# Sparse attention's distance biases stored 128 times and loaded row by row, the selection mask added to them on GpSimd

## What is computed

```python
score = jnp.einsum('bqh,bqhs->bqs', wi_b, s_idx)             # which keys are worth a look
score = jnp.where(causal[None], score, -jnp.inf)
_, sel = lax.top_k(score, topk)                              # 64 keys per query
bias = rel_bias[t5_bucket(jnp.maximum(dist, 0))]             # (distance q - k) -> 8 heads
logits = einsum('bqhc,bqkc->bqhk', qa_b, lat_sel) + moveaxis(bias, -1, 2)
p = softmax(where(valid, logits, -inf)); out = einsum('bqhk,bqkc->bqhc', p, lat_sel)
```

## Time and profile before

| | |
|---|---|
| time, three runs | 1334.58, 1338.58, 1341.36 us (median 1338.58) |
| the profiled execution | 1332.08 us, its span 1330.2 us |
| busy over the span | PE 1218.4 us (92%), POOL 895.9 (67%), ACT 587.5 (44%), DVE 464.8 (35%) |
| DMA | 196.60 MB, mean 148 GB/s; HBM written 1.06 MB |
| granted TensorE clock | mean 0.98 |

### The profile page before, as it was taken

The page is one execution under the profiler, slowest core; times in us unless marked ns, Lnnn a source line. Parts: engine busy times, 40 slices in busy tenths (PEclk is TensorE's granted clock), DMA queues, the critical chain, the costliest instruction groups (busy, mean ns, idle before and its releaser), DMA issues.

```text
span 1330.2 us, 19675 instructions
## 1 busy us (share of the span) xinstructions
PE 1218.4 (92%) x7628; PEld 1033.3 (78%) x7628; DVE 464.8 (35%) x834; ACT 587.5 (44%) x859; POOL 895.9 (67%) x913
## 2 busy tenths in 40 slices
PE   2998999999999999998989898898998989999997
PEld 2897987777677888788978886666778977788775
DVE  6476447643343111004265552332234032211101
ACT  2463234135536454445533335535456344644532
POOL 0689245314595888785966665468879966788785
PEclk9999799999999999999999999899999999999999
DMA  8755222323554566564633333235545634555562
GB/s 326 200 164 141 65 69 92 97 80 111 172 164 149 181 189 190 174 188 113 190 111 101 114 119 110 81 127 159 190 147 153 198 119 143 156 181 186 174 189 97
DMA packets 182909, 196.60 MB, mean 148 GB/s; under 512 B 7416, under 2 KB 141856, under 8 KB 182688
## 3 DMA queue, kind: packets, MB, share of 16 engines
q1 hardware_dynamic: 178336, 186.56, 45.5%
q10 hardware_dynamic: 4480, 8.78, 2.1%
HBM read 194.25 MB, written 1.06 MB: 147 GB/s over the span
## 4 chain that ended last, share of the span: by engine, by line
PE 72%; DVE 10%; POOL 6%; ACT 6%; issue 4%; DMA 1%; POOLq 0%; ACTq 0%; DVEq 0%; SPq 0%
PE ps L621 19%; PE ps L623 18%; PE ps L622 18%; PE ps L618 14%; POOL wlo L2421 6%; PE ps L626 3%; DVE hE L1693 3%; DMA raw<-in_ada_w 1%; ACT hE L1183 1%; ACT L1183 1%; ACT whi L1183 1%; DVE gt L1693 1%; DVE x L1701 1%; DVE AD L2254 1%; DVE acc L1701 0%
## 5 line engine op out<-in xcount | busy, mean ns | idle before, releaser
L2421 POOL TENSOR_TENSOR wlo<-raw,whi 128x256 fp32r<-128x256 f32 (+1 forms) x904 | 890.4, 1018 | 419.2 <-ACT whi L1183 415.0
L1183 ACT ACTIVATE whi<-raw 128x1024 fp32r<-128x1024 f32 x325 | 341.5, 1056 | 353.2 <-PE ps L623 330.5
L621 PE MATMUL ps<-whi,hThi 128*128 128x512 f32 (+2 forms) x672 | 270.0, 402 | 9.7 <-POOL wlo L2421 4.3
L623 PE MATMUL ps<-whi,hTlo 128*128 128x512 f32 (+2 forms) x672 | 261.2, 389 | 0.0
L622 PE MATMUL ps<-wlo,hThi 128*128 128x512 f32 (+2 forms) x672 | 260.8, 388 | 0.0
L621 PE MATMUL ps<-hThi,whi 128*128 128x256 f32 x576 | 171.4, 298 | 8.5 <-DVE hTlo L1693 2.6
L622 PE MATMUL ps<-hTlo,whi 128*128 128x256 f32 x576 | 165.6, 287 | 0.0
L623 PE MATMUL ps<-hThi,wlo 128*128 128x256 f32 x576 | 165.2, 287 | 0.0
L621 PEld LDWEIGHTS ps<-whi,hThi 128*128 128x128 f32 x672 | 128.6, 191 | 39.5 <-issue 13.2
L623 PEld LDWEIGHTS ps<-whi,hTlo 128*128 128x128 f32 x672 | 128.7, 191 | 26.7
L622 PEld LDWEIGHTS ps<-wlo,hThi 128*128 128x128 f32 x672 | 128.8, 192 | 22.3
(11 more groups left out here) (357 smaller groups left out, 1599.0 us busy)
## 6 DMA issues: line engine op xcount, KB each, us to landing
raw<-in_w_in SPq DMA_DIRECT2D x121, 512.0 KB, 3.6
raw<-in_ffn_w_in SPq DMA_DIRECT2D x176, 256.0 KB, 3.0
raw<-in_ffn_w_down SPq DMA_DIRECT2D x44, 512.0 KB, 4.3
raw<-in_ada_w SPq DMA_DIRECT2D x24, 512.0 KB, 5.2
raw<-in_w_mkv SPq DMA_DIRECT2D x16, 512.0 KB, 3.9
raw<-in_w_o SPq DMA_DIRECT2D x8, 512.0 KB, 3.5
raw<-in_w_branch_a SPq DMA_DIRECT2D x8, 512.0 KB, 3.7
raw<-in_w_branch_b SPq DMA_DIRECT2D x8, 512.0 KB, 3.6
```

Of the source, the lines that this page charges most:

```text
L621: e.matmul(o, l[0], r[0], start=start, stop=False)
L623: return e.matmul(o, l[1], r[0], start=False, stop=stop)
L1183: return e.activation(o, i, f, **k)
L2421: p = e.tensor_tensor(wlo[c % NHL][:, o], raw[i % NRAW][:, o], whi[c % NHL][:, o], ALU.subtract)
```

## The change

Three things are done. The DRAM scratch grows from (8, 384) to (128, 8, 384), and the store writes the same 8 rows 128 times. The two loads read partition p from copy p, starting at 255 - 128 t - p, so that the rows stand the right way up. The product with `flip` is gone, and with it PE's wait for the bias loads. GpSimd gets a `dsa` chain of its own: four tensor_tensor instructions add the mask `wk[t]` in place to `hk[t]`, four heads at a time (128 x 512 for t = 0, 128 x 1024 for t = 1), at step 13 and step 22. DVE adds `hk[t]` instead of the mask to the logits, behind a wait for GpSimd; its wait for the second mask at the head of the attention goes.

```diff
-        bias_dram = nc.dram_tensor("bias_scratch", (8, 384), F32, kind="Internal").ap()
+        bias_dram = nc.dram_tensor("bias_scratch", (128, 8, 384), F32, kind="Internal").ap()
...
-                    w.wait_ge(S["hk"], "hk")
-                    mm(o, qabs[:, h, t * 128:t * 128 + 128], latT[:, 0:n], True, False)
-                    return mm(o, C("flip"), hk[t][:, h, :], False, True)
+                    return mm(o, qabs[:, h, t * 128:t * 128 + 128], latT[:, 0:n])
...
-                e.dma_start(bias_dram, biasv).then_inc(S["bias_out"].tick("out", by=16), 16)
+                e.dma_start(bias_dram.rearrange("q h n -> h q n"), biasv.unsqueeze(1).broadcast_to([8, 128, 384])).then_inc(S["bias_out"].tick("out", by=16), 16)
...
-                    e.dma_start(hk[t][:, :, :], bass.AP(bias_dram.tensor, 128 * (1 - t), [[1, 128], [384, 8], [1, n]])).then_inc(
+                    e.dma_start(hk[t][:, :, :], bass.AP(bias_dram.tensor, 255 - 128 * t, [[8 * 384 - 1, 128], [384, 8], [1, n]])).then_inc(
...
-                               mask(t).unsqueeze(1).broadcast_to([P, 2, n]), ALU.add).then_inc(s.tick((ch, "z", g, t, h0)), 1)
+                               mask(t, g + h0), ALU.add).then_inc(s.tick((ch, "z", g, t, h0)), 1)
...
-                w.wait_ge(s, ("k", 1))
+                def mask(t, h):
+                    w.wait_ge(S["ds_g"], (t, h // 4))
+                    return hk[t][:, h:h + 2, :]
...
+            def dsa():
+                for t, before in ((0, 12), (1, 9)):
+                    for _ in range(before):
+                        yield
+                    w.wait_ge(S["hk"], "hk")
+                    w.wait_ge(S["ds_v"], ("k", t))
+                    for h in (0, 4):
+                        o = hk[t][:, h:h + 4, :]
+                        e.tensor_tensor(o, o, wk[t][:, :].unsqueeze(1).broadcast_to([P, 4, 128 * (t + 1)]), ALU.add).then_inc(
+                            S["ds_g"].tick((t, h // 4)), 1)
```

More of the change, by code:

```diff
@@ L421 @@
            "turn_a", "norm_pe", "norm_a", "norm_v", "bias_pe", "bias_v", "rw_pe", "rw_v", "rw_a", "h0_pe", "h0_v", "h0_a",
-           "h0_g", "h1_pe", "h1_v", "h1_a", "h1_g", "ds_pe", "ds_v", "ds_a", "toh_pe", "toh_a", "hg_pe", "hg_v", "hg_a",
+           "h0_g", "h1_pe", "h1_v", "h1_a", "h1_g", "ds_pe", "ds_v", "ds_a", "ds_g", "toh_pe", "toh_a", "hg_pe", "hg_v", "hg_a",
            "hg_g", "fx_pe", "fx_v", "fx_a", "ml_pe", "ml_v", "ml_a"]
@@ L2189, in values @@
                     tt(y, PS[bank_of["ds", "y", h]][p0:p0 + 64, 0:256], y, ALU.mult).then_inc(s.tick(("y", h)), 1)
-                w.wait_ge(s, ("k", 1))
+                def mask(t, h):
+                    w.wait_ge(S["ds_g"], (t, h // 4))
+                    return hk[t][:, h:h + 2, :]
                 w.wait_ge(S["ev_v"], ("zb1",))
-                yield from attention("ds", lambda t: wk[t][:, :], lambda h: values(h - 1) if h else None, *dsa_bufs)
+                yield from attention("ds", mask, lambda h: values(h - 1) if h else None, *dsa_bufs)
                 values(7)
@@ L2200, in outs, with mask @@
                     cp(Z["qb"][:, h, :], PS[bank_of["fx", "o", h]][:, 0:256]).then_inc(S["fx_v"].tick(("o", h)), 1)
-                yield from attention("fx", lambda t: mask256 if t else C("causal"), outs, *fox_bufs)
+                def mask(t, h):
+                    return (mask256 if t else C("causal")).unsqueeze(1).broadcast_to([P, 2, 128 * (t + 1)])
+                yield from attention("fx", mask, outs, *fox_bufs)
             def to_h(name, gen):
@@ L2438, in hgrn @@
                     yield
-            chains = {"head0": head(0), "head1": head(1), "hgrn": hgrn()}
+            def dsa():
[8 more added lines that the diff above has]
+                            S["ds_g"].tick((t, h // 4)), 1)
+                for _ in range(len(COST["dsa"]) - 21):
+                    yield
+            chains = {"head0": head(0), "head1": head(1), "hgrn": hgrn(), "dsa": dsa()}
             for what, *d in order:
```

## The result

The changed kernel takes 1354.84 us (median; 1350.09 to 1357.94) beside 1339.91 us of the kernel before on the same chip (1334.58 to 1341.36): ratio 1.0113, 95% interval 1.0082 to 1.0144. It is slower by 14.9 us. The forecast was 1352, range 1333 to 1361. The profiled execution took 1353.63 us.

A forecast was written before the change was run, and what follows sets the result against it. PE bounds the attention; early, PE and POOL are both full, so a late slab costs PE fully. Profiled: 1332.1 - 5.3 + 1.2 + 17 = 1345.0 (+12.9); median: 1338.6 + 12.9 = 1351.5, forecast 1352, range 1333 to 1361.

The forecast's parts named there:

- The store is late by about 30 us: Early stage, from 72.5 us: the 1.57 MB store from partitions 0 to 7 takes about 30 us, shaded from 34.
- hidden store: Rival, early stage: the store takes 10 us, slab 12's load lands in time, total 1334.5 us; chance 0.2.
- The load behind it is 18 us late: Slab 12's weight load gets turns after three quarters of the store, 16 to 18 us late, reaching PE in full.
- The clock behind the wait: After PE's early wait for the late slab, PE restarts at a lower granted clock: 2 us more.
- DVE's backlog: Early stage: DVE works off its backlog while PE waits for the late slab, giving back 2 us.
- The flip products, -5.3: Attention: dropping the 16 flip products saves their whole PE time, 5.3 us.
- DVE held up by GpSimd, +1.2 us on PE: Step 13, 227.6 to 230.4 us: GpSimd's additions delay DVE's W by 2 to 2.5 us, costing PE 1.2 us.
- DVE's addition, 0: DVE's addition to the logits: same operand sizes, 0.69 us for 128x512, so nothing added (-0.1 to +0.1 us each).
- Step 22, hidden: GpSimd's additions of 2 x 2.4 us end near 270 us, 13 us before DVE needs them: no cost.
- The new hk loads, hidden: The new loads of hk carry as many packets as the old and are hidden until 227 us.
- ACT waiting at `bias_load`: Rival: weight loads pass beside the store and ACT waits ahead of slab 15's rounding; +5, 1343.6 us; chance 0.1.
- The middle store of 15 us: Rival: the store takes 15 us, slab 12's load is 4 us late, sum 0, total 1338.7 us; chance 0.15.

The follow-up runs named there:

- e3: Changed kernel with the bias table on 128 partitions, but the store reads eight rows on partitions 0, 9, 18 to 63, each written 128 times: 1333.64 us, ratio 0.9963.
- e2: Changed kernel with the bias table made on all 128 partitions, each storing 8 copies, the same bytes: 1333.03 us, ratio 0.9969.
- e1: Kernel before with only the store made large, 128 copies from partitions 0 to 7; old loads and flip products stay: 1355.69 us, ratio 1.0133.
- e5: Kernel before with only the store enlarged, to 64 copies from partitions 0 to 7: 1340.86 us in one run.
- e11: The changed kernel once more, unaltered: 1358.10 us.
- e10: Kernel before with only the store enlarged, to 96 copies from partitions 0 to 7: 1355.96 us in one run.
- e8: Kernel before without the 16 flip products and PE's wait for hk, leaving the distance biases out: 1327.56 us in one run.
- e7: e2 with GpSimd's additions cut into instructions of 256 columns, at the same steps: 1327.75 us in one run.

## Why the prediction was right

*The store is late by about 30 us: right in kind, a little too short.* It took 31.9 us, not 30. The early term was 19.0 us from slab 8 to slab 24, 20.0 of wait and one caught up, against 17 in the sum (16 to 18, +2, -2). The nearest row in kind, the old store's 46 GB/s, was the right price, and the shading from 34 to 30 us "because the stretch contains start and end" was twice too much. The measured rate is 1.57 MB / 31.9 us = 49 GB/s. The other row, 10 us by the hk loads' engine time, is the price of the same bytes from partitions that don't crowd, as e3's 10.5 us shows; it was the price of the rival "hidden store". That rival's time, 1334.5, is that of e2 and e3 to within 1.5 us.

*The load behind it is 18 us late: right to within some 2 us, by luck, with a false rule.* I took from the earlier trace rows that a load gets its turns at three quarters of what is ahead of it. With 128 packets an engine that is at 96, near 97 us in this trace; it began at 57, 87.19. Since it went one for one from there and has 64 packets an engine of its own, the load ended with the store, near 105, and not much later or sooner than by the rule: 57 + 64 packets of the store are 121 of 128. At 64 or 32 copies the rule would have said something else. The hk loads themselves don't fit the count of 57 either; 95 an engine had gone by 98 us, when the load behind them had had 16 packets on 16 engines. What the count depends on is open. The runs have it only behind packets of 1536 bytes.

*The clock behind the wait:* forecast 0.53 and +2 us, less 2 for DVE's backlog. The clock was indeed low when PE started again at 109.15, until 112.5. But the row from which the +2 was priced is the kernel before's own low stretch of the same length, with PE just as busy, and after has no second one there. Before, then after:

```profile
110.40:113.80 3.40, 3.40 (x18) 3.40 (x18) 0.50 (x1) 0.44 (x1) 3.40 (x6) 0.50 0.76 219
```

```profile
109.10:112.50 3.40, 3.35 (x16) 3.38 (x17) 3.30 (x4) 0.65 (x1) 3.40 (x5) 0.50 0.62 175
```

So the difference owes nothing to the clock here, and the +2 was a charge for what before pays too. From slab 8 to slab 24 the loss differs from the wait by -1.0 us in after, -0.4 in e1, -0.2 in e5, -0.1 in e11 and +1.0 in e10: of the backlog at most one microsecond comes back. The two terms of the sum cancelled, which is why their errors don't show.

*The flip products, -5.3:* it lies within the 4.3 to 5.8 us that like against like gives. In the profiled execution 3.7 came, for the clock. That e8 shows 5.5 is partly luck: it had no low stretch where before had a short one.

*DVE held up by GpSimd, +1.2 us on PE:* 0.33 + 0.84. The operation that met the additions was x from TB and not W, and it was held 2.1 us, the forecast's 2 to 2.5; W came late through it. The Trainium skill (SBUF — State Buffer, "Who interferes with whom") has the two blocking each other for the whole instruction, by which the sum would have had 3 us. That the block lasts a GpSimd instruction the traces bear out, with 2.1 against 1.0 us when the instructions are halved. But only one pair of DVE met it, and the three operations that would make 3 us on PE weren't there.

*DVE's addition, 0:* 691/692/692 as in the earlier trace rows. *Step 22, hidden:* 12.1 us to spare of the 13 forecast. *The new hk loads, hidden:* landed by 123.

*The rivals.* ACT waiting at `bias_load` fell: ACT issued the loads at 113.80, 8.8 us after the store had ended, because the weight load did not pass the store and ACT itself came late. The middle store of 15 us did not occur, though e5's 15.9 us shows what it would have done: a wait of 5.96 us, where the rival had 4. The Trainium skill (SBUF — State Buffer, "Door 1: The DMA port swizzle") has partitions 0 to 7 on two ports of 27 GB/s, which makes an estimate of 29 us, and 2 more with the fixed cost that the page gives; the trace agrees, with 31.9 from the first packet to the last. By the same table partitions 0, 9, 18 up to 63 lie on eight ports; there e3's store took 10.5 us.

*The sum and the median.* 0.5 at slab 8 + 19.0 + 1.5 for the longer low clock before slab 36 + 1.2 - 3.7 = 18.5 us, and at slab 132 the table has 18.6. The terms that were forecast make 16.5 of it, for +12.9. Against the profiled execution the forecast was 1345.0, and that execution took 1353.63, 8.6 us more; that the median came within 3 us of 1352 is in part luck. The median rose by 14.9, less than the 21.6 between the two profiled executions: a typical pair differs from the profiled one. Part of this is the later stages: between slab 132 and 276 after loses 1.5 us, the same kernel in e11 loses 6.2, and e7 gains 0.9, with nothing changed there. The granted clock from 828 to 868 is 0.83 in after, and in the same work of e11 it is 0.79:

```profile
828.40:868.40 40.00, 33.19 (x121) 24.32 (x121) 11.93 (x19) 17.31 (x32) 19.29 (x28) 0.83 0.34 98
```

```profile
828.20:868.20 40.00, 33.19 (x116) 24.18 (x116) 11.59 (x19) 17.42 (x31) 19.48 (x28) 0.79 0.32 92
```

By the medians of the timed runs the account is: store alone +17.8 us (e1), everything else -3.8 to -5.0 (e2 and e3: 0.9969 and 0.9963 of 1336.86 are -4.1 and -4.9), together 13 to 14. The two forecast terms -5.3 + 1.2 = -4.1 are met in sum, and the store's 17 by 17.8.

## What to carry to other kernels

A row that is stored many times is priced by where it lies: from a few neighbouring partitions each packet cost three times what it cost from partitions further apart, and the matmul that writes the table to all partitions cost nothing that shows. A long DMA on one queue is also the lateness of every load that is issued behind it on another one if they share engines, so ask which load comes next and how much slack its slab has, and look for it in the row of one issue, not in the median. And compare executions slab by slab up to the stage in question, starting ahead of the change, since a clock that falls behind an untouched wait can hide a third of a gain.

## What the runs showed of the hardware

- Packets of 1536 bytes from partitions 0 to 7: 217 ns each on 8 engines, 49 GB/s. From partitions 0, 9 up to 63, also on 8 engines: 67 ns, 150 GB/s. From all 128, on 16: 75 ns, 310 GB/s.
- A load of SP's queue issued 0.4 us behind the start of such a store got no packet on the shared engines until 455 to 459 of the store's had gone (57 an engine, 14 us), and then one for one; in three sizes of the store alike. Behind the fast stores it was 476 on 8 engines (59.5 an engine, 3.9 us, e3) and 1001 on 16 (62.6 an engine, 4.7 us, e2): a count, not a time.
- A DVE operation with two operands in SBUF was held up beside GpSimd's additions by about 1.05 us with 512 columns, and 0.5 with 256; two of GpSimd's instructions of 512 columns took 2.70 to 2.73 us with and without that pair beside them.
- Behind one and the same PE wait of 2.7 us the granted clock stayed at 1.00 in some executions and at 0.53 for six microseconds in others, worth up to 2 us. With PE busy throughout, the same work before slab 36 met a low clock for 13.7 us in some executions and 17.1 in others, worth 1.5 us.
